# A hybrid attention and SwiGLU layer: values computed transposed for pairs of heads, a ring of five rows of logits, and the input projection moved beside the global heads

## The reference, cut to what matters

```python
h = rms_norm(x, g_pre_mix) * (1 + sc1) + sh1
qa, ka, va, cq, ckv, kidx, widx = split(h @ w_in)       # 512,128,128,256,128,64,4 = 1220 columns
out_a = sliding_window_sink_attention(qa, ka, va)       # 8 heads of 64, two chunks of 64 keys
cq = rms_norm(cq); qb, qidx = cq @ w_uq, cq @ w_qidx
kb, vb = split(rms_norm(ckv) @ w_ukv)                   # one key and value head of 64
score = sum_h widx_h * relu(qidx_h @ kidx.T)            # visible keys only
idx = top_k(score, 256)
out_b = softmax(qb @ kb[idx].T / 8 - slope * dist) @ vb[idx]   # 8 heads
x = x + gt1 * rms_norm(concat(out_a, out_b) @ w_o, g_post_mix)
h2 = rms_norm(x, g_pre_ffn) * (1 + sc2) + sh2
x = x + gt2 * rms_norm((silu(h2 @ w_gate) * (h2 @ w_up)) @ w_down, g_post_ffn)   # d_ff 2816
```

## Time and profile before

| | us |
|---|---|
| median of 3 runs | 3282.39 (3280.31 to 3283.53) |
| the profiled execution | 3280.21 |
| its span, first to last instruction | 3278.4 |
| TensorE busy | 2893.9 (88%) |
| VectorE busy | 1689.7 (52%) |
| ScalarE busy | 1569.7 (48%) |
| GpSimd busy | 315.7 (10%) |
| mean granted TensorE clock | 0.929 of 2.4 GHz |

### The profile page before, as it was taken

One profiled execution on the slowest core, in us unless ns is written; L12 is line 12 of the kernel. 1 busy time (PEld: TensorE's weight loads), 2 busy tenths in 40 slices (PEclk: granted clock), 3 DMA queues, 4 the chain that ended last, 5 costly groups with the idle time before them and its releaser, 6 DMA issues. The chain is left out here.

```text
span 3278.4 us, 42244 instructions
## 1 busy us (share of the span) xinstructions
PE 2893.9 (88%) x14392; PEld 2338.0 (71%) x14392; DVE 1689.7 (52%) x3088; ACT 1569.7 (48%) x3006; POOL 315.7 (10%) x989
## 2 busy tenths in 40 slices
PE   6678888787887888789898999999999999999997
PEld 2456666666676667678786887888877887888876
DVE  2246768586878868834454443254424443254422
ACT  0457787778777786875333222232223222232222
POOL 0112222212121120120111000000000000000000
PEclk8788888898988888889998999999999999999999
DMA  5000000000000010211465333343334333343323
GB/s 209 8 22 14 23 14 17 11 13 13 14 4 14 14 55 4 110 55 62 138 179 179 95 97 90 122 142 96 97 121 135 102 96 90 122 142 96 99 88 108
DMA packets 286884, 254.86 MB, mean 78 GB/s; under 512 B 8685, under 2 KB 238617, under 8 KB 286617
## 3 DMA queue, kind: packets, MB, share of 16 engines
q1 hardware_dynamic: 282584, 236.32, 23.3%
q10 hardware_dynamic: 4160, 16.78, 1.3%
HBM read 219.50 MB, written 33.57 MB: 77 GB/s over the span
## 5 line engine op out<-in xcount | busy, mean ns | idle before, releaser
L2002 ACT ACTIVATE p_hi<-raw 128x1024 fp32r<-128x1024 f32 x264 | 279.4, 1058 | 691.3 <-PE dbank L1972 352.4
L2079 DVE TENSOR_TENSOR p_lo<-raw,p_hi 128x1024 fp32r<-128x1024 f32 x264 | 323.4, 1225 | 429.6 <-ACT p_hi L2002 429.6
L1322 DVE TENSOR_SCALAR_CACHE_REDUCE above<-score,cand 128x384 uint8<-128x384 f32 (+6 forms) x224 | 315.8, 1410 | 4.3
L1172 ACT ACTIVATE signs<-score,pick 128x512 int8<-128x512 f32 (+6 forms) x224 | 304.4, 1359 | 28.1 <-POOL pick L684 19.7
L1150 ACT ACTIVATE logit<-tbank 128x512 f32<-128x512 f32 (+3 forms) x448 | 214.2, 487 | 209.0 <-PE tbank L903 205.8
L903 PE MATMUL tbank<-ident,logit 128*128 128x128 f32 x1336 | 249.5, 300 | 65.9 <-ACT logit L1140 57.0
L919 PE MATMUL obank<-vb,logit 128*128 128x64 f32 x2176 | 298.5, 282 | 0.0
L1970 PE MATMUL dbank<-p_hi,a_hi 128*128 128x512 f32 x704 | 277.8, 395 | 17.0 <-DVE a_lo L2106 13.8
L919 PEld LDWEIGHTS obank<-vb,logit 128*128 128x128 f32 x2176 | 292.1, 207 | 0.0
L1953 PE MATMUL gbank<-x_hi,p_hi 128*128 128x512 f32 x704 | 275.8, 392 | 14.8 <-DVE p_lo L2079 14.8
L788 PE MATMUL work<-w_in,h_T 128*128 128x512 f32 (+1 forms) x768 | 281.3, 514 | 0.7 <-ACT h_T L981 0.7
(11 more groups left out here) (216 smaller groups left out, 5115.6 us busy)
## 6 DMA issues: line engine op xcount, KB each, us to landing
raw<-in_w_gate_up SPq DMA_DIRECT2D x176, 512.0 KB, 3.8
raw<-in_w_down SPq DMA_DIRECT2D x88, 512.0 KB, 3.7
w_in<-in_w_ada ACTq DMA_DIRECT2D x4, 4096.0 KB, 13.3
wada<-in_w_ada SPq DMA_DIRECT2D x4, 2048.0 KB, 15.7
row<-in_x SPq DMA_DIRECT2D x16, 512.0 KB, 3.9
mixT<-oT SPq DMA_DIRECT2D x32, 256.0 KB, 2.3
x_rows<-in_x SPq DMA_DIRECT2D x16, 512.0 KB, 4.7
x<-x_rows SPq DMA_DIRECT2D x16, 512.0 KB, 3.1
```

What stands on the lines that cost most here:

```text
L1172: nc.scalar.activation(signs[:, 0:L], score[:, b % 2, 0:L], ACT.Sign, scale=-1.0, bias=pick[:].bitcast(F32), accum_out=less_more[:]).then_ ...
L1322: link(nc.vector.tensor_scalar(above[:, 0:L], score[:, b % 2, 0:L], cand[:].bitcast(F32), None, ALU.is_ge, ALU.add, accum_out=count[:]), b ...
L2002: nc.scalar.activation(p_hi[:, s], raw[:, s], ACT.Copy).then_inc(panel_high, 1)
L2079: nc.vector.tensor_tensor(p_lo[:, s], raw[:, s], p_hi[:, s].bitcast(F32), ALU.subtract).then_inc(panel_ready, 1)
```

## The change

- **Values.** `weighted_values` handles two heads together. The 64 value columns become the stationary operand, and the transposed probabilities of 128 queries move; the first head of the pair writes to partitions 0 to 63 of the output bank, the second to 64 to 127. The number of instructions is the same. The output comes out transposed. The groups of a pair are computed at the even head four later, and the last one, where there are several, at the odd head behind it.
- **Sums.** `invert_totals` on VectorE inverts the sums and spreads them over 512 columns, `turn_totals` transposes them on TensorE, `copy_totals` copies them on ScalarE, and `scale_output` multiplies them into oT. `turn_output`, `copy_output` and o_norm are gone.
- **Rows.** Five rows of logits with 1,920 keys take the place of four with 2,048, in a buffer of their own, which w_o uses later. w_in has its own buffer; block 15, with 2,048 keys, has its rows in it and in one row of scores. The load of w_o waits for the values of block 14 and no longer for the last `mod`.
- **Order.** From iteration 1 on, the local heads have beside them gains, latent and latent_up of block b+3 and the norm and transposes of block b+4, and global heads 0 to 4 have the five parts of the projection of block b+4. Iteration 0 is the passage.
- **Passes.** The weights of local heads fall: on VectorE from 4.5 and 3.0 to 3.2 and 2.1, on ScalarE from 1.8 to 1.1. Counted from the plan, local heads of block 10 have 8 instead of 10 passes on ScalarE and 4 instead of 5 on VectorE, global heads of block 8 have 13 instead of 11 steps of the search on VectorE and 8 instead of 7 on ScalarE, local heads of block 11 have 8 instead of 10 on VectorE and 3 instead of 4 on ScalarE, global heads of block 9 have 14 instead of 13 and 14 instead of 12; local heads of block 15 have 6 instead of 8 on VectorE.
- **Waits in mixing.** A tie step waits for a projection's squares (`lat_ssq`) and no longer for a norm's. ScalarE's norm waits for `bias_ready`, which its transposes did before.
- **Feed-forward.** The down product begins when all but the last two activation tiles are done, and waits for those before panel 11. The split of the next chunk's input is spread over the last panels. In the last chunk the last panel is computed tile by tile (`last_product`), and squares, root, scaling, addition and store follow for each tile (`last_tile`); the gains are multiplied into the first half beforehand, and the tiles go to four buffers.

```diff
     scoring = it + 2 < NB and h <= 3
     if kind == "A":
-        return (0.0 if it == b - 2 else 1.0 if h == 3 else 4.5) if scoring else 3.0
+        return (0.0 if it == b - 2 else 0.7 if h == 3 else 3.2) if scoring else 2.1
...
     if kind == "A":
-        return 0.0 if it == b - 2 and h <= 3 else 1.8
+        return 0.0 if it == b - 2 and h <= 3 else 1.1
...
+        if nxt:
+            for c in range(1, len(key_chunks("B", nxt))):
+                put(("A", c - 1), ("scores", nxt, c))
+            put(("A", 2), ("queries", "B", b))
...
+            put(("A", 0), ("gains", f))
+            put(("A", 4), ("latent", f))
+            put(("A", 6), ("latent_up", f))
+            put(("B", 0), ("queries", "A", f))
+            if g < NB:
+                put(("A", 5), ("norm", g))
+                put(("A", 7), ("transposes", g))
+                for c in range(5):
+                    put(("B", c), ("proj", g, c))
+        if b in (NB - 3, NB - 2):
+            put(("B", 1), ("mod", 2 * (b - NB + 3)))
...
+        for kind, of in (("A", nxt), ("B", b)):
+            for h in range(HEADS if of is not None else 0):
+                at = (b, kind, h)
+                steps.append(("head", kind, of, h, tuple(vector.get(at, ())), tuple(scalar.get(at, ()))))
+                add(*slots.get((kind, h), []))
...
+    def values_done(self, i):
+        pairs = self.heads[0:i // 2 * 2 + 1:2]
+        return sum(-(-len(key_tiles(kind, b)) // 4) for kind, b, _ in pairs)
...
         N_W = 8
+        def row(i):
+            k = i % RING
+            if plan.heads[i][0:2] != ("B", NB - 1):
+                return shared.later.rows[:, k * ROW:(k + 1) * ROW]
...
             def first_loads():
-                sp.wait_ge(work_full, plan.work0["mod", MODS - 1] + 1)
+                sp.wait_ge(pv_done, plan.values_done(plan.head_no["B", NB - 2, HEADS - 1]))
                 for k in range(KD):
                     sp.dma_start(shared.later.w_o[:, k, :], w["w_o"][k * P:(k + 1) * P, :]).then_inc(shared.later.wo_in[k], 16)
...
+            def turn_totals(i):
+                kind, b, h = plan.heads[i]
+                t = plan.turned_totals(i)
+                pe.wait_ge(rtotal_ready, OUT_ORDER.index((kind, b)) + 1)
+                if t >= 2:
+                    pe.wait_ge(pt_ready, t - 1)
+                for j in range(4):
+                    mm = nc.tensor.transpose(tbank[t % 2][:, j * P:(j + 1) * P], rtotal_wide[:, j, :], ident[:])
+                mm.then_inc(pt_full, 1)
...
             def weighted_values(i, g):
                 kind, b, h = plan.heads[i]
                 tiles = plan.groups(i)[g]
                 last = g == len(plan.groups(i)) - 1
-                t = plan.group0[i] + g
-                pe.wait_ge(pt_ready, t + 1)
+                pe.wait_ge(pt_ready, plan.group0[i + 1] + g + 1)
                 o = OUT_ORDER.index((kind, b))
                 if g == 0 and h == 0 and o >= 2:
-                    pe.wait_ge(o_copied, o - 1)
+                    pe.wait_ge(o_made, o - 1)
                 for j, kt in enumerate(tiles):
-                    v = vb[:, kt, :] if kind == "B" else va[:, kt % 4, HD * (h // 4):HD * (h // 4 + 1)]
-                    mm = nc.tensor.matmul(obank[o % 2][:, h * HD:(h + 1) * HD], 
-                                          logit[:, i % 4, (4 * g + j) * P:(4 * g + j + 1) * P], v,
-                                          start=(g == 0 and j == 0), stop=(last and j == len(tiles) - 1))
+                    for r in range(2):
+                        v = vb[:, kt, :] if kind == "B" else va[:, kt % 4, HD * (h // 4):HD * (h // 4 + 1)]
+                        mm = nc.tensor.matmul(obank[o % 2][r * HD:(r + 1) * HD, h // 2 * P:(h // 2 + 1) * P], v,
+                                              row(i + r)[:, (4 * g + j) * P:(4 * g + j + 1) * P],
+                                              start=(g == 0 and j == 0), stop=(last and j == len(tiles) - 1))
                 mm.then_inc(pv_done, 1)
...
-                values = len(plan.groups(i - 3)) if 3 <= i < n + 3 else 0
-                for c in range(max(pieces, groups, values)):
+                pair = i - 5 if i % 2 else i - 4
+                values = len(plan.groups(pair)) if 0 <= pair < n else 0
+                first = max(values - 1, 1)
+                for c in range(max(pieces, groups, values, 1)):
                     if c < pieces:
                         piece(i, c)
+                    if c == 0 and i % 2:
+                        for g in range(first, values):
+                            weighted_values(pair, g)
+                    if c == 0 and 4 <= i < n + 4 and plan.heads[i - 4][2] == HEADS - 1:
+                        turn_totals(i - 4)
                     if c < groups:
                         transpose_group(i - 2, c)
-                    if c < values:
-                        weighted_values(i - 3, c)
-                if 5 <= i < n + 5:
-                    turn_output(i - 5)
+                    if i % 2 == 0 and c < min(first, values):
+                        weighted_values(pair, c)
...
-                    if b + 3 < NB:
-                        dve.wait_ge(x_ssq, b + 4)
-                    else:
-                        dve.wait_ge(lat_ssq, NB)
+                    dve.wait_ge(lat_ssq, min(b + 4, NB))
...
+            def invert_totals(i):
+                kind, b, h = plan.heads[i]
+                if h < HEADS - 1:
+                    return
+                o = OUT_ORDER.index((kind, b))
+                dve.wait_ge(exp_done, i + 1)
+                sums = total[:, o % 2, :]
+                if kind == "A":
+                    link(nc.vector.tensor_tensor(sums, sums, exp_sink[:, o % 2, :], ALU.add))
+                link(nc.vector.reciprocal(rtotal[:], sums))
+                if o:
+                    dve.wait_ge(o_stored, 16 * o)
+                nc.vector.tensor_copy(rtotal_wide.rearrange("p j (r d) -> p (j r) d", d=HD),
+                                      rtotal[:].unsqueeze(2).to_broadcast([P, HEADS, HD])
+                                      ).then_inc(rtotal_ready, 1)
...
-                dve.wait_ge(pv_done, plan.group0[i + 1])
-                sums = total[:, o % 2, :]
-                if kind == "A":
-                    link(nc.vector.tensor_tensor(sums, sums, exp_sink[:, o % 2, :], ALU.add))
-                link(nc.vector.reciprocal(rtotal[:], sums))
-                if o:
-                    dve.wait_ge(o_turned, o)
-                nc.vector.tensor_tensor(o_norm[:], obank[o % 2][:].rearrange("p (h d) -> p h d", d=HD),
-                                        rtotal[:].unsqueeze(2).to_broadcast([P, HEADS, HD]),
-                                        ALU.mult).then_inc(o_scaled, 1)
+                dve.wait_ge(pv_done, plan.values_done(i))
+                dve.wait_ge(pt_ready, plan.turned_totals(i) + 1)
+                nc.vector.tensor_tensor(oT[:], obank[o % 2][:].rearrange("p (j t) -> p j t", t=P), rtotal_T[:],
+                                        ALU.mult).then_inc(o_made, 1)
...
+            def last_product(c, n, s, m):
+                pe.wait_ge(panel_ready, c * PANELS + UP + n + 1)
+                for t in range(TPC):
+                    for i in range(2):
+                        wh, wl = p_hi[:, s, i * HALF:(i + 1) * HALF], p_lo[:, s, i * HALF:(i + 1) * HALF]
+                        ah = a_hi[:, m * 2 + i, t * P:(t + 1) * P]
+                        al = a_lo[:, m * 2 + i, t * P:(t + 1) * P]
+                        nc.tensor.matmul(dbank[t][:], ah, wh, start=False, stop=False)
+                        nc.tensor.matmul(dbank[t][:], ah, wl, start=False, stop=False)
+                        mm = nc.tensor.matmul(dbank[t][:], al, wh, start=False, stop=(i == 1))
+                    mm.then_inc(tile_done, 1)
...
-                pe.wait_ge(act_ready, (c + 1) * KF + 2)
+                pe.wait_ge(act_ready, (c + 1) * KF)
                 if not first:
                     pe.wait_ge(out_made, c * TPC)
                 for n in range(2 * DOWN):
                     m = n % DOWN
-                    down_product(c, n, n % 2, m, m == 0, m == DOWN - 1, refill=(n == DOWN))
+                    if n == DOWN - 1:
+                        pe.wait_ge(act_ready, (c + 1) * KF + 2)
+                    if last and n == 2 * DOWN - 1:
+                        last_product(c, n, n % 2, m)
+                    else:
+                        down_product(c, n, n % 2, m, m == 0, m == DOWN - 1, refill=(n == DOWN))
...
-                    panel_high_part(c, KF + DOWN - 1, s)
+                for q in range(DOWN - 2, DOWN):
+                    for s in range(2):
+                        if not last:
+                            x_high_part(c + 1, 2 * (q - DOWN + 2) + s)
+                        panel_high_part(c, KF + q, s)
                 if not last:
                     for s in range(2):
...
+                                            ).then_inc(half_gained, 1)
```

(18 more changed lines are left out.)

196 lines of the change are left out of this document (109 added, 87 removed).

## The result

The changed kernel takes 3311.09 us (median of 4 runs, 3306.09 to 3312.29) for 3281.69 of the kernel before in the same runs: 1.0086 times as long, 95% interval 1.0069 to 1.0104. The forecast was 3160, in a range from 3100 to 3240. The profiled execution took 3311.5 us, its span is 3309.7.

A forecast was written before the change was run, and what follows sets the result against it. No engine fills mixing; the bound changes twice in each iteration. From 3280.2 us it took 77 for iterations 0 to 12, 18.5 for the last blocks, 28.3 for feed-forward: 3156.4, by the median 3159, predicted 3160, range 3100 to 3240.

The forecast's parts named there:

- The density carried over: Local stretches: busiest engine's time over 0.96, as VectorE in block 15, gives 31 for 34.6 and 29.6 for 36.0 us.
- The latents: First local stretch: latent, latent_up and norm add 6.4 us to ACT; the latent part adds 2.5 to PE.
- Rival 1: Local stretch: transposes wait for the norm's chain ending in GpSimd's shift, up to 6 us an iteration; 3209 to 3225; chance 0.20.
- Rival 3: Projection adds 11.5 us to each global stretch, local ones shrink only 3.6 and 6.4; 3310 us; chance 0.08.
- Rival 2: Values: the array's two halves don't run together, a pair's group costs 2.07 for 1.62 us; 3234 us; chance 0.07.
- Values: Values in pairs: a full group costs 1.16 instead of 1.62 us, 63 us less PE work at full clock.
- Block 15's gain: Global heads of block 15: PE is the bound, -6 us, and the drain at the end another -2.
- blocks 13 and 14: Their global heads: PE has 12.6 us less work and is busy 84%, so -7.5 us.
- the wait of an odd head: An odd head's row waits for the pair's last group, delaying DVE 1.2 us, hidden unless DVE is the bound.
- The local heads of block 15: DVE-bound, with two passes fewer, which two global stretches take up: -3 us.
- Global stretches: The first takes some 54 us for 54.9, two engines at 50; the second 59 for 65.5.
- Feed-forward: Down product's waits 13.8 us, low clock after stalls 5, tile-by-tile end 9.5: -28.3 us in sum.

The follow-up runs named there:

- e7: The changed kernel with latent and latent_up back beside global heads 2 and 4, projection parts at global heads 1, 1, 4, 5, 5; 3366.5 us, ratio 1.0270.
- e22: The changed kernel with latent_up behind global head 2 instead of local head 6; 3291.0 us, ratio 1.0034.
- e20: The changed kernel with transposes behind global head 2 instead of local head 7, projection parts behind global heads 3, 3, 4, 5, 5; 3360.7 us, ratio 1.0249.
- e8: The changed kernel with the norm of block b+4 behind local head 2 instead of 5; 3308.3 us, ratio 1.0091.
- e5: The changed kernel with the old order, passes and waits, and a pair's last values group moved into the even head; 3250.1 us, ratio 0.9911.
- e3: The kernel before with only the changed feed-forward part; 3247.1 us, ratio 0.9908.
- e12: e3 with eight idle transposes added in each global head of blocks 1 to 12; 3262.0 us, ratio 0.9950.
- e9: The changed kernel with ten idle transposes added in each local head of blocks 3 to 15; 3346.9 us, ratio 1.0203.

## Why the prediction was wrong

**The density carried over.** This is the step that failed. Dividing the engines' sums by 0.96, from VectorE in block 15, gave 31 and 29.6 us for local 10 and 11; measured are 40.3 and 41.9, densities of 0.79 and 0.75. The sums were low too, and are the smaller part: ACT 29.7 us forecast and 32.0 measured in local 10, DVE 28.3 and 31.6 in local 11. The passes didn't leave these stretches as counted from the plan: ScalarE runs 9 in the window of local 10 and VectorE 10 in that of local 11, where the forecast had 8 and 8 and the kernel before runs 10 and 10. With the measured sums 0.96 would give 33.3 and 32.9, so of the 9.3 and 12.3 us missed the density holds 7.0 and 9.0. e7 shows that even an emptier local stretch takes 34.3 us in the mean, and 35.1 and 37.0 in these two. Before the change TensorE was 91% busy there, but it was not alone what kept the stretch long; the projection filled gaps of a chain of round trips, and taking it away left the gaps. The last paragraph of the prediction named this as its weak point and gave it no weight in the range.

**The latents.** With the norm they were priced as busy time, 6.4 us of ACT and 2.5 of PE. Their price was where they stand in TensorE's order: the two last local heads grew by 5.7 us, waiting on two banks and copies a head late. e22 gives 20 us of it back in all, and e20 takes 53 of the local stretches' 67 us away and pays more elsewhere.

**Rival 1**, the shift, was seen as described, 32.4 us in 11 places, and worth nothing: e8 removed it and another wait of the same instructions took its place. **Rival 3** named the time, 3310, and the growth of iterations 0 to 12, 75 for 73.2, but by luck: its sum lets two global stretches grow by 23 us and two local ones shrink by 10. Global stretches became shorter by 14 us, not longer; local ones grew by 67, and the passage by 20.0. The sum did not count iteration 0 by itself: it has one projection more in iteration 0 beside heads that had no room for it. **Rival 2** fell: a pair's group of 16 takes 1.03 us, from 1612.59 to 1613.62.

```profile
1612.59 1.09 PE L970 MATMUL obank<-w_in,vb 128*64 128x128 f32 x16
1613.62 0.66 PE L941 MATMUL tbank<-ident,w_in 128*128 128x128 f32 x4
```

**Values.** The size was right: 1.03 us a full group for 1.16, and 65 us less of TensorE's busy time (e5 against e3) for 63. The worth was wrong. Block 15's gain was 3.7 of 6 in seven heads, and 5.8 of 8 with the drain; blocks 13 and 14 together gave 0.6 of 7.5. The sentence that called the wait of an odd head hidden unless VectorE is the bound failed: in the old order e5 took it away and gained 13 us. The local heads of block 15 gave 2.9 of 3.

**Global stretches** were forecast at 54 and 59 us; they are 54.0 and 64.9. The first is right by luck in part: the two engines taken at 50 us are busy 46.7 (DVE) and 47.9 (PE). In the second the sums came out, ACT 51.3 us for 53.5 and PE 50.4 for 52 at a clock that did rise to 0.92, but the density is 0.79 for the 0.91 that the forecast had: the same failed step. TensorE waits 7.2 us there for ScalarE's copies of the scores.

**Feed-forward.** -28.3 forecast, -32.4 measured (e3): 11.1 for 9.5 at the end, the 13.8 of stalls as counted, and 7.5 for the 5 of the clock. The clock bears that out in kind: over 14 us at each of the four starts of a down product it was 0.88, 1.00, 0.76 and 0.76 before, and 1.00 at all four in the changed kernel. This was the only part in which one engine is the bound throughout, and there sums of its rows were good to a few us.

## What to carry to other kernels

A stretch in which one engine is 91% busy needn't be bound by it. Before its work is moved away, take it out in one run and see whether the stretch shortens: e7's local stretches, 412 us for 419.5, would have warned of this forecast. Adding idle work, as in e12 and e9, is a weaker test, since it raises the clock too. Side work that passes through few banks and is copied a head later is dear when two of its steps stand side by side; two heads between them brought two local heads back from 13.9 to 9.3 us in e20, but what was moved cost more where it went, so time the whole. Where a wait is to be removed, look which other wait of the same instruction ends next. And split the change: e3 alone is the best version measured, 0.9908 (0.9891 to 0.9925), better than before and after; e5 can't be told from it.
